# Delta rule on one core: the sample group's products of states moved to the first two turns, its new states made in two parts, and the last token tile normed by halves of its channels

## The reference, cut to what matters

```
def step(S, inp):
    r_t, w_t, k_t, v_t, kk_t, b_t = inp
    sa = jnp.einsum('bhvk,bhk->bhv', S, kk_t)
    S = S * w_t[:, :, None, :] - sa[..., None] * b_t[:, :, None, :] + v_t[..., None] * k_t[:, :, None, :]
    return S, jnp.einsum('bhvk,bhk->bhv', S, r_t)
...
S_fin, ys = lax.scan(step, wkv0.astype(f32), seq)      # prompt: from zero; sample: from state_wkv (8 sequences)
...
m = jnp.mean(y, -1, keepdims=True)                      # group norm by head, bonus, gate, w_out
...
xp = layer_norm(ALPHA * xp + dp, ln_g[i], ln_b[i])
xs = layer_norm(ALPHA * xs + ds, ln_g[i], ln_b[i])
```

## Time and profile before

| what | us |
|---|---|
| median of 3 runs | 1483.42 (1481.92 to 1490.57) |
| the profiled execution, its own time | 1485.49 |
| its span, first to last instruction or transfer | 1483.7 |
| PE busy | 1415.4 (95%) |
| DVE busy | 798.1 (54%) |
| ACT busy | 578.4 (39%) |
| POOL busy | 242.3 (16%) |

### The profile page before, as it was taken

The page is one execution under the profiler, slowest core; times in us unless marked ns, Lnnn a source line. Parts: engine busy times, 40 slices in busy tenths (PEclk is TensorE's granted clock), DMA queues, the critical chain, the costliest instruction groups (busy, mean ns, idle before and its releaser), DMA issues. The chain is left out here.

```text
span 1483.7 us, 37543 instructions
## 1 busy us (share of the span) xinstructions
PE 1415.4 (95%) x16154; PEld 1284.7 (87%) x16154; DVE 798.1 (54%) x1592; ACT 578.4 (39%) x1182; POOL 242.3 (16%) x343
## 2 busy tenths in 40 slices
PE   7999999999999799999999989999999999998997
PEld 6989898887899799999999848899999997665885
DVE  6737245777821377777777564561111222775545
ACT  6626246887821122221222332441111132886324
POOL 0000000000000355654566230000001000214000
PEclk9999999999999999999999899999999998999999
DMA  5724122567692245434553146024334236431202
GB/s 205 223 59 103 59 89 89 161 174 225 193 261 87 59 110 117 107 86 108 117 117 89 53 149 229 29 78 145 91 98 116 67 119 168 150 103 33 87 29 93
DMA packets 244294, 173.47 MB, mean 117 GB/s; under 512 B 148735, under 2 KB 218303, under 8 KB 243215
## 3 DMA queue, kind: packets, MB, share of 16 engines
q1 hardware_dynamic: 212167, 156.12, 36.6%
q10 hardware_dynamic: 31968, 15.04, 3.5%
HBM read 110.97 MB, written 60.46 MB: 116 GB/s over the span
## 5 line engine op out<-in xcount | busy, mean ns | idle before, releaser
L366 PE MATMUL mix_acc<-mix_high,mix_w_high 128*128 128x364 f32 (+1 forms) x768 | 177.3, 339 | 11.5 <-ACT mix_high L432 10.3
L366 PE MATMUL mix_acc<-mix_low,mix_w_high 128*128 128x364 f32 (+1 forms) x768 | 171.5, 332 | 1.2 <-DVE mix_low L586 1.2
L366 PE MATMUL mix_acc<-mix_high,mix_w_low 128*128 128x364 f32 (+1 forms) x768 | 170.4, 330 | 0.0
L366 PEld LDWEIGHTS mix_acc<-mix_high,mix_w_high 128*128 128x128 f32 x768 | 129.6, 188 | 30.4 <-issue 28.6
L366 PEld LDWEIGHTS mix_acc<-mix_low,mix_w_high 128*128 128x128 f32 x768 | 132.5, 189 | 2.3 <-DVE mix_low L586 2.1
L366 PEld LDWEIGHTS mix_acc<-mix_high,mix_w_low 128*128 128x128 f32 x768 | 133.1, 188 | 0.2 <-DVE mix_w_low L600 0.2
L1482 PE MATMUL out_acc<-qkvg_room_r_high,qkvg_room_w_high 128*128 128x364 f32 (+1 forms) x320 | 105.8, 331 | 2.1 <-DVE qkvg_room_w_low L1834 2.1
L600 DVE TENSOR_TENSOR mix_w_low<-mix_wt,mix_w_high 128x1024 fp32r<-128x1024 f32 x32 | 39.2, 1224 | 124.9 <-ACT mix_w_high L438 124.6
L1482 PE MATMUL out_acc<-qkvg_room_r_low,qkvg_room_w_high 128*128 128x364 f32 (+1 forms) x320 | 105.1, 329 | 0.0
L1482 PE MATMUL out_acc<-qkvg_room_r_high,qkvg_room_w_low 128*128 128x364 f32 (+1 forms) x320 | 105.1, 329 | 0.0
L1832 DVE CAST qkvg_room_w_high<-qkvg_room_wt 128x1024 fp32r<-128x1024 f32 x20 | 14.0, 700 | 155.4 <-DMA qkvg_room_wt<-in_w_att 155.4
(11 more groups left out here) (278 smaller groups left out, 3418.3 us busy)
## 6 DMA issues: line engine op xcount, KB each, us to landing
mix_wt<-in_w_in SPq DMA_DIRECT2D x32, 512.0 KB, 4.6
qkvg_room_wt<-in_w_att SPq DMA_DIRECT2D x20, 512.0 KB, 3.7
delta_bk<-scr_bk SPq DMA_DIRECT2D x17, 512.0 KB, 4.7
delta_kr<-scr_kr SPq DMA_DIRECT2D x17, 512.0 KB, 7.1
scr_kr<-mix_outs SPq DMA_DIRECT2D x16, 512.0 KB, 3.8
scr_bk<-mix_outs SPq DMA_DIRECT2D x16, 512.0 KB, 4.5
early_xpad<-in_xpad SPq DMA_DIRECT2D x8, 548.5 KB, 8.8
scr_xg<-early_xs SPq DMA_DIRECT2D x8, 544.0 KB, 3.0
```

The lines of the kernel that those rows point to most:

```text
L366: mm = pe.matmul(acc[:, s, k, 0:width], w[:, s, d, :], r[:, d, n0:n0 + width], start=d == 0 and q == 0, stop=d == DT - 1 and q == 2)
```

## The change

- The loads of `s_sample` move from turns 1 to 8 of `delta_rule` to jobs 27 to 30 of the projections (`follow_slowly`), and the sample chunk's `kr` is loaded into a tile of its own, `kr_own`, in job 26. It shares memory with the second inverse, so `solve_blocks(1)` now waits for `own_made`.
- `turn_states` takes a list of pairs: pairs 0 and 1 at the end of turn -1, pairs 2 to 4 in turn 0 behind the first two grams, pairs 5 to 7 in turn 0 behind `turn_rows(1, 0)`. It writes the `wide` and `chain` banks. ACT's two copies to `own_turned` go to turn 0.
- POOL scales one pair of `s_sample` at the end of each of the turns 1 to 8.
- `v_own` is made by POOL, 8 instructions at the end of turn 15, ahead of `end_state(15)`; `u_own` is made by ACT alone, 8 instructions.
- `make_own_states` is cut in `own_values` (the `v_own` part, which opens the bank) and `own_updates` (the `u_own` part, which closes it). Pairs 0 and 1 have their values around `make_z(16)`, pairs 2 and 3 behind `make_u(16)`; pairs 4 to 7 have both parts together behind `make_y(16)`.
- `turn_y(15)` moves from ahead of `make_u(16)` to behind it and the values of pairs 2 and 3; `turn_y(16)` to behind the last pair. On DVE, the first four adds are put between the steps of the last group norm, and `gate_y(16)` behind the last add.
- In `out2` the last tile's mean and variance come from DVE's `bn_stats` over each half and `bn_aggr`; ACT does only the root; centring, scaling and the store are done by halves of 512 channels. `out1` is as before.

```diff
@@ mixed_projections, SP @@
+                    if G_ * DT + 2 < n < G_ * DT + 7:
+                        for pair in range(2):
+                            follow_slowly(sp, 2 * (n - (G_ * DT + 3)) + pair)
@@ first_of_delta @@
+        sp.dma_start(d["kr_own"][:], scr["kr"][TILES, :, :, :, 0:NB * NT]).then_inc(d["kr_own_loaded"], 16)
+    def load_states(sp, pair):
+        sp.dma_start(d["s_sample"][:, pair], a["s_sample"][:, pair]).then_inc(d["s_loaded"], 16)
@@ delta_rule, POOL @@
-                    if i == SAMPLE:
-                        pool.wait_ge(own_made, 2)
-                        for pair in range(DT):
...
+                    if front == SAMPLE:
+                        pool.wait_ge(v_loaded[SAMPLE % 3], 16 * (SAMPLE // 3 + 1))
+                        for b in range(NB):
+                            own = seq_mask[:, b:b + 1].rearrange("p (j n) -> p j n", j=1).broadcast_to([128, DT, 64])
+                            pool.tensor_tensor(v_own[:, b], v_rows[:, SAMPLE % 3], own, ALU.mult).then_inc(v_owned, 1)
+                    if 1 <= i <= DT:
+                        pair = i - 1
+                        pool.wait_ge(own_made, 2)
+                        end = keep["ends_sample"][:, pair, :].rearrange("p (b o) -> p b o", o=1).broadcast_to([128, NB, 64])
+                        pool.tensor_tensor(s_sample[:, pair], s_sample[:, pair], end, ALU.mult).then_inc(own_ended, 1)
@@ delta_rule, PE @@
+                def own_values(pairs):
+                    if pairs[0] == 0:
+                        pe.wait_ge(solved_wide, SAMPLE + 1)
+                        pe.wait_ge(rows_kept, 2 * SAMPLE + 2)
+                        pe.wait_ge(v_owned, NB)
+                    for pair in pairs:
+                        if pair >= 4:
+                            pe.wait_ge(own_done, pair - 3)
+                        for p in HALVES:
+                            pe.matmul((lm_bank + grown_bank)[pair % 4][p, :], rows[p, SAMPLE % 2, 1, pair, :], v_own[p, :, pair, :], start=True, stop=False)
+                def own_updates(pairs):
+                    if pairs[0] == 0:
+                        pe.wait_ge(u_owned, NB)
...
                     if live(behind):
                         make_u(behind)
+                    if behind == SAMPLE:
+                        own_values((2, 3))
+                        turn_y(SAMPLE - 1)
...
+                    if i == 0:
+                        turn_states((2, 3, 4))
...
-                    if i == SAMPLE:
-                        turn_states()
                     if behind == SAMPLE:
-                        make_own_states()
+                        own_updates(range(4))
+                        for pair in range(4, DT):
+                            own_values((pair,))
+                            own_updates((pair,))
+                        turn_y(SAMPLE)
...
+                    if i == 0:
+                        turn_states((5, 6, 7))
...
+                    if i == -1:
+                        turn_states((0, 1))
@@ delta_rule, ACT @@
+                    if i == 0:
+                        keep_own(0)
...
-                        for b in range(NB // 2):
+                        for b in range(NB):
@@ delta_rule, DVE @@
                     if behind == SAMPLE:
+                        add_own((0, 1))
                         sum_squares(behind)
                         invert_root(behind)
+                        add_own((2, 3))
                         scale_y(behind)
+                        for pair in range(4, DT):
+                            add_own((pair,))
+                            if pair == DT - 1:
+                                gate_y(SAMPLE)
+                            for d in range(2 * pair - DT, 2 * pair - DT + 2):
+                                ahead["rest_of_weights"](dve, d)
@@ project_and_norm, DVE, last tile of out2 @@
+                    dve.wait_ge(added, ROW_TILES)
+                    moments(0)
+                    add_rows(1, t)
+                    dve.wait_ge(added, 2 * ROW_TILES)
+                    moments(1)
+                    dve.wait_ge(last, 2)
+                    dve.bn_aggr(row_stats[:], halves_stats[:]).then_inc(last, 1)
...
+                    scale_half(0)
+                    centre_half(1)
+                    scale_half(1)
```

More of the change, by code:

```diff
@@ L1191, in make_own_states @@
+                def own_values(pairs):
[3 more added lines that the diff above has]
+                        pe.wait_ge(v_owned, NB)
+                    for pair in pairs:
                         if pair >= 4:
                             pe.wait_ge(own_done, pair - 3)
-                        for k, operand in enumerate((u_own, v_own)):
-                            for p in HALVES:
-                                mm = pe.matmul(bank[pair % 4][p, :], rows[p, SAMPLE % 2, k, pair, :], operand[p, :, pair, :], start=k == 0, stop=k == 1)
+                        for p in HALVES:
+                            pe.matmul((lm_bank + grown_bank)[pair % 4][p, :], rows[p, SAMPLE % 2, 1, pair, :], v_own[p, :, pair, :], start=True, stop=False)
@@ L1196, in make_own_states @@
+                def own_updates(pairs):
+                    if pairs[0] == 0:
+                        pe.wait_ge(u_owned, NB)
+                    for pair in pairs:
+                        for p in HALVES:
+                            mm = pe.matmul((lm_bank + grown_bank)[pair % 4][p, :], rows[p, SAMPLE % 2, 0, pair, :], u_own[p, :, pair, :], start=False, stop=True)
                         mm.then_inc(own_s, 1)
@@ L1694, in _ @@
                 act.wait_ge(eps_set, 1)
-                for t in range(ROW_TILES):
+                for t in range(ROW_TILES if follow is not None else TILES):
                     sum_row(t)
@@ L1699, in _ @@
                     square_row(t)
+                if follow is None:
+                    act.wait_ge(last, 3)
+                    act.activation(root[:, TILES:ROW_TILES], row_stats[:, 1:2], ACT.Sqrt, bias=eps[:]).then_inc(rooted, 1)
                 if follow is not None:
```

129 lines of the change are left out of this document (70 added, 59 removed).

## The result

The changed kernel took **1474.62 us** (median of 10 runs, 1468.99 to 1478.38), the kernel before 1484.57 us beside it (median of 10, 1481.92 to 1490.57). The ratio is 0.9925, with a 95% interval of 0.9905 to 0.9945: 0.75% faster. The forecast was 1476.1 us, the gain 7.3 us; measured are 10 to 11 (9.95 by the medians, 11.1 by the ratio). The profiled execution took 1477.48 us, its span 1475.7 us.

What follows compares the result with a forecast made beforehand. TensorE was taken to bound nearly everything, except turn 0's waits and the chain ending the delta rule. Terms -11.0 + 3.2 + 0.8 - 0.3 = -7.3 gave a median of 1476.1 us, range 1470.5 to 1482.5.

Steps and rivals of the forecast that it cites:

- its sign: End of make_y(15) to next stage: 30.3 us where it was 41.3; over 36 would mean the prediction is wrong.
- The end: Turn 16 to the next stage: starts at 867.1 instead of 878.07, 11.0 us saved.
- All of it arises ahead of u: Turn 16: the whole 11.0 us saving comes before u's copy, at 844.25 instead of 855.35.
- Turn 0: Products of states: pairs 0 to 4 hidden in PE's waits, pairs 5 to 7 cost in full, +3.2 us.
- The loads: Eight states and kr_own loaded in jobs 26 to 30 on SP's queue: nothing for PE, all landing before 490.
- POOL in turns 1 to 8: One more product of about 1.25 us per turn: counted as nothing, 10 us if the state's add waits.
- Restart: First matmuls of out1 after PE's longer stand: +0.8 us, between 0 and 2.
- can only: Start of out1: a longer stand of PE can only lengthen the low-clock stretch, +0.8 us, between 0 and 2.
- Tail: Last add to the end, with bn_stats and halves: -0.3 us, from -1.6 to +1.1.
- the clock holds in turn 0: Turn 0: products fill the wait and keep 2.4 GHz, up to 2.4 us return, 1473.7 us; chance 0.20.
- POOL is slow: Turn 16: v_own at 1.49 each ends 2.7 us later and delays z, 1478.8 us; chance 0.10.

Runs made afterwards that it cites:

- e9: Changed kernel with the values' matmuls of pairs 0 to 3 moved from around z and u to behind u_own; ratio 0.9950 to the kernel before.
- e11: Changed kernel with the last y turned ahead of pair 6 on PE and gated ahead of pair 6's add on DVE; ratio 0.9923 to the kernel before.
- e6: Changed kernel with POOL's state_end(15) ahead of v_own and both values of pairs 0 and 1 behind z; ratio 0.9906 to the kernel before.
- e3: Changed kernel with new states made whole as before: v_own on ACT, u_own on ACT and DVE, turn_y(15) ahead of u; ratio 0.9949 to before.
- e1: Kernel before with only the eight loads of the sample sequences' states moved from turns 1 to 8 into the projections; ratio 0.9998 to before.
- e2: Changed kernel with products of states, their two copies and POOL's scalings put back into turn 16, loads still early; ratio 0.9996 to before.

## Why the prediction was right, and where it wasn't

The mechanism and the sign were right: the gain arises in turn 16, where the products of states go, and turn 0 pays part of it back. The size was 7.3 for a measured 10 to 11. That the forecast of the time itself is only 1.5 us off is in part luck: it was counted from 1483.42 for before, which was 1484.57 in the end. From PE's end of `make_y(15)` to the next stage are 28.5 us, where the prediction named 30.3 as its sign and over 36 as being wrong. Term by term:

- **The end, forecast -11.0, traced -12.7 (-13.3 against the mean of two traces of before).** By its steps, from turn 16's `spread_blocks`: `v_own` was to end after 7.2 us and ended after 6.4, since POOL took 1.06 each and not 1.15. u was to be copied after 14.6 and was after 13.6. From there the forecast's distances held to the last update (15.6 us, both), and DVE's instructions there, 0.60 between starts, brought the y store another 0.8 forward. The distance from that store to the next stage was exact, 4.04.
- **"All of it arises ahead of u"** holds as to the place (12.1 of 12.7 us). Behind u two things offset each other, as the prediction said: from the first update to the last matmul of the new states PE needs 10.5 us for 14.7, and from there to the next stage pass 6.6 us for 2.9. The runs price them: the early values are worth 3.05 (e9), and the late y store costs 1.9 (e11), where the forecast blamed DVE's adds and the store together. What the prediction gave no price is the order of PE's list ahead of u. It took for granted that `turn_y(15)` is out of the way; with the products gone and the old order the end is 40.27, for 35.73, and 3.5 of this is u coming later. Against e6, in which z is copied at the same place (10.44 us into the stretch), u comes even 4.2 later. In the kernel before, the same order cost 0.7 at most (`make_u` starts 23.91 us into the stretch, z's copy ends at 23.25), since the products and z kept PE busy while y(15) was normed. The three prices, 3.5 and 3.05 less 1.9, make 4.65, and e3 lies 4.54 above the changed kernel. The clock is part of the 3.5: it held where `turn_y(15)` stands behind u, but for 3.4 us in e9.
- **Turn 0, forecast +3.2.** The 96 records cost 2.93 in their row and 2.8 between the usual forms, 22.24 and 19.45. The first trace showed +3.7, since its clock was low for 10 us, and where PE has no wait. In three of ten traces the products of pairs 0 and 1, priced at nothing, stand in a stretch that took 1.5 us more at the lower clock; that they cause it isn't shown.
- **The loads, forecast 0.** In the traces -4 in turns 1 to 4, which the times of e1 and e2 don't confirm. Whether anything was left out here stays open.
- **POOL in turns 1 to 8, forecast 0 (up to 10 us).** Turns 1 to 4 got shorter and turn 5 to 15 are within the others' spread: nothing.
- **Restart, forecast +0.8:** 6.55 for the 16 matmuls against 5.71 in the first traces, +0.8, but 5.70 in the second of the changed kernel, +0. PE stood for 7.11 us ahead of it in both, where it stood for 4.02, so the longer stand did not always lengthen the slow part, as the prediction's "can only" would let one think.
- **Tail, forecast -0.3:** -0.2.
- **Rival "the clock holds in turn 0".** The second grams did run at full clock (1.07 for 1.97), as that rival had it, but in the first trace a fall at 516 took the gain back. The low clock of turn 0 is (1 - 0.79) / 0.5 x 24.05, 10 us. The rule of the Trainium skill ("TensorE: Matmul & The Clock Gate", Part 1) that the clock is throttled by default and released by activity would make turn 0 with no wait the one with the highest clock. The traces disagree: 24.05 us busy of 24.05 at 0.79, but 0.92 in the second trace, where PE was busy for 21.08 of 22.24. In turn 16 they agree: the clock fell in e3's stand of 4.16 us and held in the changed kernel, whose waits between `make_y(15)` and the last update are 0.55 us at most. The rule gives the direction at the one place and not at the other.
- **Rival "POOL is slow".** The contention of which the Trainium skill speaks ("GPSIMD Engine Reference", table of hardware facts) is there, but DVE paid for it: its product of two SBUF tensors took 1.54 beside `v_own` for the 0.69 of the earlier trace rows, on no critical path, while POOL kept 1.06.

By the means of two traces of each kernel, the span got 12.1 us shorter: the stretch ahead of turn 0 +1.4, turn 0 +3.2, turns 1 to 4 -4.75, turns 5 to 15 +1.2, the end -13.3, the rest +0.1. That is more than the 10 to 11 of the runs because the two traced executions of before lay 2.3 us above their medians in the mean, and those of the changed kernel 0.2 below. So the turns other than 0 are read with a doubt of some microseconds, while the end repeats: 35.73 in all four traces with its code unchanged.

## What to carry to other kernels

Before a long run of small matmuls is costed, look at what its clock does: moved out of a chain it gives back its own length and the slow work behind it, and moved into a wait it costs nothing only as far as the wait is still there when the work ahead runs at half clock. When long work leaves a chain, look again at the order of what stood behind it: `turn_y(15)` ahead of `make_u` was hidden before, and in e3, with the products gone, u came 3.5 us later. And follow the last store of a stage by its issue: here the next stage began 4.04 us behind it, and moving it ahead of two adds was worth 1.9 us, until DVE's last instruction set the start.

## What the runs showed that was not expected

PE was granted 1.2 GHz while it was busy without a gap: 5.00 of 5.00 us at 0.50 in the products of states of e2, 4.00 of 4.00 at 0.53 in turn 0 of the changed kernel. With the products in it, turn 0 comes in two lengths and none between, 22.24 and 24.05 to 24.16, by whether its first grams run at the lower clock. Without the products it is the other way round: 20.33 with the first grams at full clock (1.96), 19.43 to 19.47 in the three traces in which they took 3.09 to 3.48, and with that the wait behind them shrank from 3.91 to 2.3 us.
